# Three quarters of a second feed-forward product from seven half-size products, and the row root applied before the square

## What is computed

```python
        hn = rmsnorm(h, norm2_g[l])
        h = h + jnp.square(jax.nn.relu(hn @ w_ff1[l])) @ w_ff2[l]
    return rmsnorm(h, final_g)
```

## Time and profile before

| | |
|---|---|
| median of 3 runs | 1214.16 us (1211.78, 1214.16, 1214.39) |
| profiled execution, first to last instruction (span) | 1212.6 us |
| mean granted TensorE clock | 0.993 of full |
| PE matmuls busy | 1168.3 us (96%) |
| POOL busy | 680.5 us (56%) |
| DVE busy | 649.7 us (54%) |
| ACT busy | 315.6 us (26%) |

### The profile page before, as it was taken

The page is one execution under the profiler, slowest core; times in us unless marked ns, Lnnn a source line. Parts: engine busy times, 40 slices in busy tenths (PEclk is TensorE's granted clock), DMA queues, the critical chain, the costliest instruction groups (busy, mean ns, idle before and its releaser), DMA issues.

```text
span 1212.6 us, 18634 instructions
## 1 busy us (share of the span) xinstructions
PE 1168.3 (96%) x6792; PEld 946.3 (78%) x6792; DVE 649.7 (54%) x1196; ACT 315.6 (26%) x666; POOL 680.5 (56%) x610
## 2 busy tenths in 40 slices
PE   8999999998999999999899999999999999999996
PEld 6777787777887887877777777778888888888885
DVE  3887555887824575543877768572544200335022
ACT  3125022124732233212135455310312000113001
POOL 4885244444546686665634433376666666666662
PEclk9999999999999999999999999999999999999998
DMA  7221111114013222224521111123232323333321
GB/s 240 95 90 53 54 53 53 36 54 139 2 42 105 70 87 87 72 81 137 203 73 53 36 53 53 52 83 92 87 104 86 104 89 102 93 97 119 90 87 69
DMA packets 29683, 102.39 MB, mean 84 GB/s; under 512 B 3632, under 2 KB 6064, under 8 KB 28848
## 3 DMA queue, kind: packets, MB, share of 16 engines
q1 hardware_dynamic: 27232, 93.47, 24.6%
q10 hardware_dynamic: 2384, 7.99, 2.1%
HBM read 95.16 MB, written 2.10 MB: 80 GB/s over the span
## 4 chain that ended last, share of the span: by engine, by line
PE 83%; DVE 7%; POOL 3%; ACT 3%; issue 3%; DMA 1%; DVEq 0%; SPq 0%; POOLq 0%; ACTq 0%
PE acc L280 23%; PE acc L282 21%; PE acc L281 21%; POOL w_lo L1688 3%; PE aux L1762 3%; PE aux L789 2%; PE aux L779 2%; PE aux L1743 1%; PE aux L347 1%; PE acc L501 1%; PE aux L919 1%; PE aux L770 1%; PE aux L769 1%; DMA residual<-x 1%; PE aux L699 0%
## 5 line engine op out<-in xcount | busy, mean ns | idle before, releaser
L1680 POOL CAST w_hi<-w_raw 128x1024 fp32r<-128x1024 f32 x164 | 177.0, 1080 | 485.0 <-issue 349.5
L1688 POOL TENSOR_TENSOR w_lo<-w_raw,w_hi 128x256 fp32r<-128x256 f32 x352 | 295.9, 870 | 7.1
L280 PE MATMUL acc<-ht_hi,w_hi 128*128 128x512 f32 x672 | 272.2, 405 | 5.5 <-POOL w_lo L1688 2.2
L282 PE MATMUL acc<-ht_hi,w_lo 128*128 128x512 f32 x672 | 264.7, 394 | 0.0
L281 PE MATMUL acc<-ht_lo,w_hi 128*128 128x512 f32 x672 | 264.2, 393 | 0.0
L1683 POOL TENSOR_TENSOR w_lo<-w_raw,w_hi 128x1024 fp32r<-128x1024 f32 x76 | 188.0, 2473 | 6.1
L280 PEld LDWEIGHTS acc<-ht_hi,w_hi 128*128 128x128 f32 x672 | 127.4, 190 | 35.9 <-POOL w_lo L1688 6.1
L282 PEld LDWEIGHTS acc<-ht_hi,w_lo 128*128 128x128 f32 x672 | 127.3, 189 | 27.6
L281 PEld LDWEIGHTS acc<-ht_lo,w_hi 128*128 128x128 f32 x672 | 127.8, 190 | 24.2 <-issue 0.7
L280 PE MATMUL acc<-w_hi,ht_hi 128*128 128x512 f32 x256 | 105.4, 412 | 0.1
L280 PE MATMUL acc<-w_hi,ff_hi 128*128 128x512 f32 x256 | 100.4, 392 | 2.3 <-POOL w_lo L1683 2.3
(11 more groups left out here) (433 smaller groups left out, 1880.9 us busy)
## 6 DMA issues: line engine op xcount, KB each, us to landing
w_raw<-units SPq DMA_DIRECT2D x164, 512.0 KB, 3.5
cmp_w<-w_kv ACTq DMA_DIRECT2D x4, 1024.0 KB, 7.8
residual<-x SPq DMA_DIRECT2D x4, 512.0 KB, 7.0
k_turned<-k_split SPq DMA_DIRECT2D x8, 256.0 KB, 3.7
result<-normalized SPq DMA_DIRECT2D x4, 512.0 KB, 2.6
consts_sb<-consts SPq DMA_DIRECT2D x1, 1120.5 KB, 7.3
k_turned<-k_split ACTq DMA_DIRECT2D x2, 512.0 KB, 5.5
norm_post_sb<-norm_post ACTq DMA_DIRECT2D x1, 512.0 KB, 4.5
```

The costliest lines, as they stand in the source:

```text
L280: nc.tensor.matmul(bank, ah, bh, start=start, stop=False)
L282: return nc.tensor.matmul(bank, al, bh, start=False, stop=stop)
L1680: nc.gpsimd.tensor_copy(w_hi[:, slot], raw[:, j]).then_inc(hi_split, 1)
L1688: done = nc.gpsimd.tensor_tensor(w_lo[:, slot, kk, cols], raw[:, j, kk, cols], w_hi[:, slot, kk, cols].bitcast(F32), ALU.subtract)
```

## The change

The hidden units are now worked in four quarters of 1024. Of a quarter's second product, two halves of tokens, two halves of hidden units and two halves of output columns make eight block products of 256 tokens x 512 hidden units x 512 columns. For the first three quarters seven products of that size give the same sums (Winograd's form of Strassen's algorithm): the operands are the blocks themselves or sums and differences of them, and each result is added to one or two places. For the last quarter the second product is as before, two slabs of four units.

PE alternates one unit of the next quarter's first layer with one product (rounds i = 0 to 6, then a last unit). The weight blocks, 512 x 512, are loaded by SP apart from the ring; DVE forms their differences in place, ACT copies the high part (`ff_w_hi`), POOL subtracts the low part (`ff_w_lo`), into one buffer, tile by tile. Of the activations DVE forms sums, ACT the high part (`ff_a_hi`) and DVE the low part (`ff_a_lo`), into two buffers. DVE adds the products' banks (`aux`) to X or to `ff_common`.

Since the sums run over tokens of different roots, the root goes into the operand: DVE takes the rectified bank times the root's row, and ACT squares in place. So the row has to be there for the first slab.

```diff
--- before.py
+++ after.py
+QUARTERS, PRODUCTS, TILES = 4, 7, 4
...
+U_LAST = U_FF + 2 * UPS * QUARTERS
+N_LOADS = U_LAST + 2 * UPS
+SLAB_LAST = SLAB_FF + 2 * QUARTERS
+SLAB_END = SLAB_LAST + 2
...
@@ tensor queue @@
-            for j in range(1, UPS):
-                weight_unit(pe, U_FF, j, ht_hi, ht_lo, SLAB_FF, False, FLIP3)
...
-                with pe.Fori(0, FF_HALVES - f) as n:
-                    weight_slab(pe, n * FF2_UNITS + (f * U_HALF + U_FF + UPS * FF1_SLABS), ff_hi, ff_lo,
-                                n + (f * SLABS_HALF + SLAB_FF + FF1_SLABS), True, units=FF2_UNITS,
-                                operand=(on["fflo_s"], f * 16 + 1))
...
+            weight_unit(pe, U_FF, 1, ht_hi, ht_lo, SLAB_FF, False, FLIP3)
+            weight_unit(pe, U_FF, 2, ht_hi, ht_lo, SLAB_FF, False, FLIP3)
+            pe.wait_ge(flip_lo, FLIP3 + KD)
+            pe.wait_ge(diag_ready, 3)
+            nc.tensor.matmul(aux[0][:], const("ones"), diag[:], start=True, stop=True).then_inc(row_summed, 1)
+            weight_unit(pe, U_FF, 3, ht_hi, ht_lo, SLAB_FF, False, FLIP3)
+            weight_slab(pe, U_FF + UPS, ht_hi, ht_lo, SLAB_FF + 1, False)
+
+            pe.wait_ge(row_ready, 3)
+            for q in range(QUARTERS - 1):
+                for i in range(PRODUCTS + 1):
+                    slab, j = SLAB_FF + 2 * (q + 1) + i // UPS, i % UPS
+                    for b in range(4):
+                        weight_piece(pe, U_FF + 2 * UPS * (q + 1) + i, j, b, 2 * j, ht_hi, ht_lo, slab,
+                                     j == 0, j == UPS - 1, False)
+                    if i < PRODUCTS:
+                        product_on_tensor(pe, q, i)
+
+            weight_slab(pe, U_LAST, ff_hi, ff_lo, SLAB_LAST, True, operand=(on["fflo_s"], 1))
...
+        BLOCK_OF = (B11, B21, B12, B11, B22, B11, B21)
+        SUM_OF = (0, 0, 2, 1, 0, 3, 4)
...
+            return (raw_ff[:, LOW_K, EARLY_T], raw_ff[:, HIGH_K, EARLY_T], raw_ff[:, LOW_K, LATE_T], s1[:], s4[:], s2[:],
+                    raw_ff[:, HIGH_K, LATE_T])[i]
...
+        def product_on_tensor(pe, q, i):
+
+            n = PRODUCTS * q + i
+            pe.wait_ge(a_split, A_SPLIT + n + 1)
+            if n >= 2:
+                pe.wait_ge(prod_out, PROD_OUT + n - 1)
+            for k in range(TILES):
+                pe.wait_ge(p_split, P_SPLIT + TILES * n + k + 1)
+                for tt in range(2):
+                    cols = slice(tt * P, (tt + 1) * P)
+                    done = split_product(pe, aux[2 * (n % 2) + tt][:],
+                                         (a_hi[:, n % 2, k, cols], a_lo[:, n % 2, k, cols]),
+                                         (p_hi[:, k], p_lo[:, k]), k == 0, k == TILES - 1)
+                done.then_inc(prod_used, 1)
...
+        def product_high_on_scalar(act, q, i):
+
+            n = PRODUCTS * q + i
+            if SUM_OF[i]:
+                act.wait_ge(w_sum, W_SUM + 4 * q + SUM_OF[i])
+            else:
+                act.wait_ge(block_in[BLOCK_OF[i]], BLOCK_IN + 16 * (q + 1))
+            for k in range(TILES):
+                if n:
+                    act.wait_ge(prod_used, PROD_USED + TILES * (n - 1) + k + 1)
+                nc.scalar.activation(p_hi[:, k], blk[BLOCK_OF[i]][:, k], ACT.Copy).then_inc(p_high, 1)
+
+        def operand_high_on_scalar(act, n):
+
+            q, i = divmod(n, PRODUCTS)
+            if n >= 2:
+                act.wait_ge(prod_used, PROD_USED + TILES * (n - 1))
+            act.wait_ge(on["ff_squared"], KD * q + (KD if i else TILES))
+            if 2 <= i <= 5:
+                act.wait_ge(a_sum, A_SUM + 4 * q + (2, 1, 4, 3)[i - 2])
+            nc.scalar.activation(a_hi[:, n % 2], left_operand(q, i), ACT.Copy).then_inc(a_high, 1)
+
+        def squares_on_scalar(act, quarter, s):
+
+            for b in range(4):
+                act.wait_ge(acc_out[b], SLAB_FF + 2 * quarter + s + 1)
+                tile = ff[quarter % 2][:, 4 * s + b]
+                nc.scalar.activation(tile, tile, ACT.Square).then_inc(on["ff_squared"], 1)
...
@@ scalar queue @@
-                        nc.scalar.activation(ff_r[:, b], acc[b][:], ACT.Relu).then_inc(acc_out[b], 1)
-                        nc.scalar.activation(ff_hi[:, i * 4 + b], ff_s[:, b], ACT.Copy).then_inc(on["ffhi_s"], 1)
...
+            squares_on_scalar(act, 0, 0)
+            operand_high_on_scalar(act, 0)
+            product_high_on_scalar(act, 0, 0)
+            squares_on_scalar(act, 0, 1)
+            operand_high_on_scalar(act, 1)
+            for q in range(QUARTERS - 1):
+                for i in range(PRODUCTS):
+                    n = PRODUCTS * q + i
+                    if n:
+                        product_high_on_scalar(act, q, i)
+                        if n + 1 < PRODUCTS * (QUARTERS - 1):
+                            operand_high_on_scalar(act, n + 1)
+                    if i == 4:
+                        squares_on_scalar(act, q + 1, 0)
+                if q == QUARTERS - 2:
+                    act.wait_ge(p_split, P_SPLIT + TILES * PRODUCTS * (QUARTERS - 1))
+                    last_high_on_scalar(act, 0)
+                squares_on_scalar(act, q + 1, 1)
...
@@ vector queue @@
-            step(V.tensor_tensor(ff_scale, rstd, rstd, ALU.mult))
-                        V.tensor_tensor(ff_s[:, b], ff_r[:, b], ff_r[:, b], ALU.mult).then_inc(on["square_s"], 1)
-                        V.tensor_tensor(ff_lo[:, i * 4 + b], ff_s[:, b], ff_hi[:, i * 4 + b].bitcast(F32),
-                                        ALU.subtract).then_inc(on["fflo_s"], 1)
+            rstd_diagonal(step)
+            rstd_row(eng, 2)
...
+                    V.scalar_tensor_tensor(out=ff[quarter % 2][:, 4 * s + b], in0=acc[b][:], scalar=0.0, in1=R[:],
+                                           op0=ALU.max, op1=ALU.mult).then_inc(acc_out[b], 1)
...
+            def operand_low(n):
+                q, i = divmod(n, PRODUCTS)
+                eng.wait_ge(a_high, A_HIGH + n + 1)
+                V.tensor_tensor(a_lo[:, n % 2], left_operand(q, i), a_hi[:, n % 2].bitcast(F32),
+                                ALU.subtract).then_inc(a_split, 1)
...
+                    homes = ((common[:, tt], early[:, first_half]), (early[:, first_half],),
+                             (late[:, second_half], late[:, first_half]), (late[:, second_half], early[:, second_half]),
+                             (early[:, second_half],), (common[:, tt],), (late[:, first_half],))[i]
...
+                            done = V.tensor_tensor(home, home, bank, ALU.add)
...
+            def block_sum(out, plus, minus):
+                for part in (slice(0, 2), slice(2, 4)):
+                    done = V.tensor_tensor(blk[out][:, part], blk[plus][:, part], blk[minus][:, part], ALU.subtract)
+                done.then_inc(w_sum, 1)
...
+                    V.tensor_tensor(s1[:], raw_ff[:, LOW_K, LATE_T], raw_ff[:, HIGH_K, LATE_T], ALU.add).then_inc(a_sum, 1)
+                    V.tensor_tensor(raw_ff[:, LOW_K, LATE_T], raw_ff[:, LOW_K, EARLY_T], raw_ff[:, LOW_K, LATE_T],
+                                    ALU.subtract).then_inc(a_sum, 1)
...
+            relu_out(0, 0)
+            operand_low(0)
+            relu_out(0, 1)
+            for q in range(QUARTERS - 1):
+                for i in range(PRODUCTS + 1):
+                    n = PRODUCTS * q + i
+                    if i:
+                        product_out(n - 1)
+                    if i < PRODUCTS and n + 1 < PRODUCTS * (QUARTERS - 1):
+                        operand_low(n + 1)
+                    if i == 0:
+                        operand_sums(q, 0)
+                    if i == 1:
+                        first_block_sums(q)
+                    if i == 2:
+                        operand_sums(q, 1)
+                    if i == 3:
+                        relu_out(q + 1, 0)
+                        third_block_sum(q)
+                    if i == 4:
+                        last_block_sum(q)
+                if q == QUARTERS - 2:
+                    last_low(0)
+                relu_out(q + 1, 1)
...
@@ gpsimd queue @@
+            def product_low(q, i):
+                n = PRODUCTS * q + i
+                for k in range(TILES):
+                    pool.wait_ge(p_high, P_HIGH + TILES * n + k + 1)
+                    nc.gpsimd.tensor_tensor(p_lo[:, k], blk[BLOCK_OF[i]][:, k], p_hi[:, k].bitcast(F32),
+                                            ALU.subtract).then_inc(p_split, 1)
+
+            ff_split(U_FF + 2 * UPS)
+            for q in range(QUARTERS - 1):
+                for i in range(PRODUCTS + 1):
+                    if i < PRODUCTS:
+                        product_low(q, i)
+                    ff_split(U_FF + 2 * UPS * (q + 1) + i + 1)
```

More of the change, by code:

```diff
@@ L1043, in hgrn_exps_on_scalar, with last_high_on_scalar @@
+        def last_high_on_scalar(act, s):
+            act.wait_ge(on["ff_squared"], KD * (QUARTERS - 1) + TILES * (s + 1))
+            for k in range(TILES * s, TILES * (s + 1)):
```

(30 more changed lines are left out.)

178 lines of the change are left out of this document (128 added, 50 removed).

## The result

The changed kernel takes 1222.47 us (median of 7 runs, 1216.07 to 1224.93), the kernel before 1213.8 in the same job: a ratio of 1.0071, 95% interval 1.0053 to 1.0088. It is slower by 0.7%, and 0.5 us from the time forecast. The profiled execution took 1224.27 us, with a span of 1222.5. One execution of the kernel before, in the job of e0_again, took 2323.8 us; it is left out of every range and moves that job's median by 0.05 us.

What follows compares the result with a forecast made beforehand. PE was taken as the bound, busy 96% overall and throughout this stage. Terms -16.3 + 4.8 + 1.6 + 18.9 = +9.0 us, from the runs' median 1214.16, gave 1223 us; forecast 1217 to 1227 (chance 0.60), range 1208 to 1231.

Steps and rivals of the forecast that it cites:

- Matmuls: Second product, first three quarters: 7 products replace 8 units of 24 matmuls each, 16.3 us less.
- Row root: Before the diagonal's matmul: PE waits 3.9 us, held about 0.9 by the matmul; +4.8, between +2.5 and +4.8.
- 1.6 of clock: Behind each long PE wait: matmuls at half clock cost 1.6 us more, at the row root and each turn.
- the exclusion: POOL and vector instructions with both inputs in SBUF exclude each other for a whole instruction.
- First quarter: Product 2's chain of differences, cuts and split makes PE wait 3.1 us, plus 1.6 of clock: 4.7.
- Turns and the rounds behind: Two quarter turns: wait 2.9, clock 1.6, lag 2.6 in rounds 1 to 4; 7.1 us per later quarter.
- The price of a hold: Each 1024-column vector instruction with both inputs in SBUF holds POOL off 1.08 us, net 0.94.
- waits as forecast, clock never falls: Rival for the changed stage: waits come but full clock stays, 1214.5 to 1217 us; chance 0.12.
- four new stretches: Sign in the changed stage: four stretches more at half clock.
- The saving arrives: Rival: holds fall into POOL's idle time, turns and row root cost little, 1200 to 1204 us; chance 0.15.
- POOL late in every round: Rival: strided remainders and in-place sums run longer, p_lo late as well as w_lo, 1228 to 1233 us; chance 0.13.
- Loads: Weight block loads: same bytes, issued at least a product ahead, costed at nothing; one late block about 7 us.

Runs made afterwards that it cites:

- e0_again: The changed kernel run once more, nothing edited: 1218.65 us (1215.66 to 1223.96), ratio 1.0047.
- e_all: Changed kernel with diagonal on the scalar engine, its matmul inside unit 3, product 0's high parts ahead of the squares, unit casts on the scalar engine: 1198.32 us.
- first profile: Profiled execution of the changed kernel as first measured, nothing edited: 1224.27 us, span 1222.5.
- e0_third: The changed kernel a third time, nothing edited, one execution: 1218.92 us.
- e_rootact: Changed kernel with the row root's diagonal built by the scalar engine, not the vector engine: 1216.69 us, ratio 1.0027.
- e_reduce: Changed kernel with two-input vector remainders, differences and sums of quarters two and three replaced by one-input reductions (network not computed): 1203.12 us, ratio 0.9935.
- e_root: Changed kernel with the diagonal built by the scalar engine and its matmul behind the second of unit 3's four pieces: 1215.57 us, ratio 1.0018.

## Why the prediction was right, and where only by its sum

*Matmuls.* 72 fewer, 2 more, as forecast; e_all shows that the 16.3 us are real.

*Row root.* Forecast 4.8 and 1.6 of clock, 6.4 together. In the first profile TensorE is at its normal pace again 6.5 us late, in e0_third 7.7, in e0_again 2.7. The forecast took the third diagonal instruction as blocked, and named the other case as the lower end (a wait of 1.6; it is 1.69). Both happen, on a margin of some 0.01 us in POOL's start. The choice of one side was the error: the term is 6.5 or more in some executions and 2.7 in others, and within the changed stage no other difference between the three profiles of this kernel is as large. With copies on the scalar engine (e_rootact) the gap is 1.11, which agrees with the exclusion, here on instructions of 128 columns.

The Trainium skill, SBUF — State Buffer, "Who interferes with whom", lets issue order decide. The traces agree in three profiles of seven, where the third instruction got in ahead of the cast, and not in the four others, nor at 662.04: in all seven the third instruction's record starts about 0.05 us ahead of the cast's.

*First quarter.* Forecast a wait of 3.1 and 1.6 of clock; 2.91 and 1.8 in e0_again, 2.94 and 3.0 in the first profile. The chain behind this term does not add up as printed: POOL's split, 3.5 with one hold of 0.94, goes from 21.3 to 25.7, not to 25, so its own steps give a wait of 3.9. What made the printed 3.1 nearly right is POOL's four subtractions before it, which took 7.1 us in the first profile where the chain had 8.0.

*Turns and the rounds behind.* Forecast 2.9 + 1.6 + 0.8 for the turn and the round after; measured 2.84 + 0 + 2.34, or 2.84 + 1.7 + 0.73. This is the step that was mis-stated: the 1.6 us of clock was entered as a cost of its own, and it isn't one there. Behind a turn POOL is the bound for two rounds, so TensorE at half pace only comes later to a wait that it would have had anyway. The sum held because I had also subtracted it from the next round's lag (13.3 against 10.9 + 1.6). Had I believed the clock spared, that lag would have grown by as much: the rival "waits as forecast, clock never falls" (1214.5 to 1217) left this out, and its time was wrong for the two turns. A later quarter costs 6.9 us in both profiles (gaps and slow matmuls), forecast 7.1.

*The sum.* The mechanism and the stage's terms hold, but that the median came within 0.5 us is partly luck. The forecast was 9.0 above the kernel before. The first job has 8.7 between its medians, the second (e0_again) 6.1, and single executions of the changed kernel lie anywhere from 1215.66 to 1224.93.

*The price of a hold.* Forecast 0.94 us of POOL per two-input vector instruction of 1024 columns, from two rows; 1.02 over a whole quarter, by e_reduce.

The Trainium skill, TensorE: Matmul & The Clock Gate, "HAM oscillation — how this bites in real kernels", puts the idle gaps that cost the clock above those of the first quarter and the turns here (2.84 to 2.94 us). The granted clock fell behind the first quarter's 2.9 us in every profile that had it, behind the 4.02 at the row root in all four that had it, behind the 2.84 at the turns in e0_again and e0_third and not in the first profile, e_rootact or e_root, and never behind 1.11, 1.57 or 1.69. Behind the 2.47 of the last quarter it fell in five of the eleven profiles that have this gap. Of the four new stretches forecast, the three profiles of the changed kernel show two, three and four. So the traces don't agree with the rule, and the length of the wait alone does not decide. What does was not settled.

*Rivals.* "The saving arrives" fell on the holds; "POOL late in every round" did not come: rounds 2 to 4 have gaps under 0.9 us. Loads cost nothing, as put: the profile puts no wait of TensorE or POOL in this stage on a transfer.

## What to carry to other kernels

Fewer matmuls pay only if what they trade for stays off the resource that feeds TensorE: here 16.3 us of TensorE were bought with 57 vector instructions of two SBUF inputs, each of which takes 1.02 us from GpSimd, and GpSimd delivers the weights. Count such pairs per round before anything else. If a round comes out above TensorE's, move GpSimd's single-input work to the scalar engine (here it had 69% of its time free, and its casts of 1024 columns, 1.07 us in the earlier trace rows, took 1.06 in e_all, where both engines are busy, so it shows no part in the exclusion), and let what the next round needs go ahead of work that can wait. And where TensorE is behind a bound engine, as at the turns here, half clock wasn't a second cost (5.28 us with it, 5.18 without): count the lag or the clock, not both.

## What the runs showed of the hardware that I had not expected

- A race of two engines for 0.01 us (GpSimd's cast 0.69 or 0.70 us behind the vector engine's first instruction) decides whether TensorE is 6.5 to 7.7 us late or 2.7. How much of the spread of the runs it makes is not shown. The changed kernel's 14 runs lie between 1215.66 and 1224.93, the kernel before's in the same three jobs between 1208.45 and 1216.06, and e0_third, on the slow side of the race, still ended 0.9 us ahead of e0_again, on the fast side, because it came to the stage 6.0 us earlier.
- Even a vector instruction of 4 columns is held off: in the Newton steps ahead of the diagonal one takes 2.25 us beside GpSimd's subtraction, where its like takes 0.16:

```profile
865.46 2.25 DVE L433 SCALAR_TENSOR_TENSOR small<-small 128x4 f32<-128x4 f32 x1
...
868.15 0.16 DVE L433 SCALAR_TENSOR_TENSOR small<-small 128x4 f32<-128x4 f32 x1
```

- A reduction over 1024 SBUF columns (1.21 us each) leaves GpSimd alone (its cast at 1.043 us). But one input is not the whole rule: the diagonal's scalings, one tensor and a scalar per partition, do meet it. Which other operations do was not tried here.
